# Gate and up products of two feed-forwards by seven products of halves, with negated halves and adding transfers

## The reference

```python
def swiglu(h, w_gu, w_down):
    gu = h @ w_gu
    g, u = jnp.split(gu, 2, axis=-1)
    return (jax.nn.silu(g) * u) @ w_down
...
        x = x + swiglu(rms_norm_2(x, ffn_norm[l]), ffn_w_gu[l], ffn_w_down[l])
```

## Time and profile before

| | us |
|---|---|
| median of 3 runs | 1973.48 (1969.23 to 1978.84) |
| the profiled execution | 1978.27 |
| its span, first to last instruction | 1976.5 |
| busy: TensorE, weight loads | 1916.9, 1540.9 |
| busy: VectorE, ScalarE, POOL | 1328.6, 1024.8, 197.5 |

### The profile page before, as it was taken

How to read it: one execution, slowest core, us unless ns; L and a number is a source line. 1 busy time by engine, 2 the same in 40 slices (tenths; PEclk the granted TensorE clock), 3 DMA queues, 4 the chain that set the end, 5 groups by cost and what they waited for, 6 DMA issues and landing times.

```text
span 1976.5 us, 23049 instructions
## 1 busy us (share of the span) xinstructions
PE 1916.9 (97%) x8818; PEld 1540.9 (78%) x8818; DVE 1328.6 (67%) x1698; ACT 1024.8 (52%) x1562; POOL 197.5 (10%) x261
## 2 busy tenths in 40 slices
PE   5999999999999999999999999999999999999997
PEld 4768868888888888758888888887777778888886
DVE  6776699998999999863542844748445452745737
ACT  4434258888888888744332422426555542332423
POOL 4110221122211100020000000000020100000000
PEclk9999999999999999999999999999999999999999
DMA  8556479999999999962233052322221134052211
GB/s 282 165 195 217 157 262 355 377 374 379 381 366 370 362 363 366 339 205 70 64 128 128 1 192 64 110 82 78 96 64 65 43 116 131 21 192 64 83 66 43
DMA packets 200026, 366.50 MB, mean 185 GB/s; under 512 B 13514, under 2 KB 84055, under 8 KB 199914
## 3 DMA queue, kind: packets, MB, share of 16 engines
q1 hardware_dynamic: 181152, 343.20, 49.4%
q10 hardware_dynamic: 8714, 11.17, 1.7%
q0 software_dynamic: 10048, 10.62, 1.6%
HBM read 365.05 MB, written 24.65 MB: 197 GB/s over the span
## 4 chain that ended last, share of the span: by engine, by line
PE 85%; DVE 7%; DMA 3%; issue 2%; ACT 2%; POOL 1%; ACTq 0%; POOLq 0%; DVEq 0%
PE ps L361 82%; DVE wlo L306 3%; DMA raw<-in_w_expert_gate 1%; PE ps L2323 1%; DMA VR<-in_b_subln 1%; PE ps L2350 1%; ACT whi L277 1%; DMA raw<-in_w_expert_up 0%; DMA raw<-in_w_expert_down 0%; PE ps L3150 0%; DMA raw<-in_a_w_in 0%; PE ps L898 0%; DVE acc L358 0%; DVE X L2937 0%; DMA raw<-in_ada_w 0%
## 5 line engine op out<-in xcount | busy, mean ns | idle before, releaser
L306 DVE TENSOR_TENSOR wlo<-raw,whi 128x1024 fp32r<-128x1024 f32 (+1 forms) x598 | 697.8, 1212 | 228.2 <-ACT whi L277 224.6
L277 ACT ACTIVATE whi<-raw 128x1024 fp32r<-128x1024 f32 (+1 forms) x598 | 594.1, 1045 | 279.6 <-PE ps L361 248.0
L361 PE MATMUL ps<-hT3h,whi 128*128 128x512 f32 x352 | 137.2, 390 | 0.6 <-DVE hT3l L358 0.6
L361 PE MATMUL ps<-hT5h,whi 128*128 128x512 f32 x352 | 137.2, 390 | 0.6 <-DVE hT5l L358 0.6
L361 PE MATMUL ps<-hT3h,wlo 128*128 128x512 f32 x352 | 137.1, 390 | 0.0
L361 PE MATMUL ps<-hT3l,whi 128*128 128x512 f32 x352 | 137.1, 390 | 0.0
L361 PE MATMUL ps<-hT5h,wlo 128*128 128x512 f32 x352 | 137.1, 389 | 0.0
L361 PE MATMUL ps<-hT5l,whi 128*128 128x512 f32 x352 | 137.1, 389 | 0.0
L2960 DVE TENSOR_TENSOR XN<-XN,ps 128x512 f32<-128x512 f32 x44 | 30.1, 688 | 129.1 <-PE ps L361 128.5
L2892 ACT ACTIVATE XN<-ps 128x512 f32<-128x512 f32 x44 | 26.3, 597 | 164.8 <-PE ps L361 163.0
L361 PE MATMUL ps<-whi,XT1h 128*128 128x512 f32 x256 | 102.8, 402 | 1.5 <-DVE XT1l L2406 1.5
(11 more groups left out here) (491 smaller groups left out, 4183.5 us busy)
## 6 DMA issues: line engine op xcount, KB each, us to landing
raw<-in_w_expert_gate SPq DMA_DIRECT2D x64, 1024.0 KB, 7.3
raw<-in_w_expert_up SPq DMA_DIRECT2D x64, 1024.0 KB, 8.1
raw<-in_w_expert_down SPq DMA_DIRECT2D x64, 1024.0 KB, 7.2
raw<-in_ffn_w_gu SPq DMA_DIRECT2D x44, 1024.0 KB, 5.1
raw<-in_ffn_w_down SPq DMA_DIRECT2D x16, 1024.0 KB, 8.8
raw<-in_ada_w SPq DMA_DIRECT2D x24, 512.0 KB, 4.8
raw<-in_a_w_in SPq DMA_DIRECT2D x8, 1024.0 KB, 11.0
raw<-in_kv_w SPq DMA_DIRECT2D x8, 1024.0 KB, 5.2
```

The costliest lines, as they stand in the source:

```text
L277: e.activation(hi[:, c], x, ACT.Copy).then_inc(self.S("w_hi"), 1)
L306: e.tensor_tensor(lo[:, c], raws[h], hi[:, c].bitcast(F32), ALU.subtract).then_inc(self.S("w_lo"), 1)
L361: return e.matmul(o, l, r, start=start, stop=stop, skip_group_check=True)
```

## The change

The first unit of each feed-forward stays as it was. The other ten (`up`, n = 1 to 10) are done by seven products of halves too: tokens in two halves (EARLY_T, tokens 256 to 511; LATE_T, 0 to 255), the contraction of 1024 in two halves of 4 chunks, and columns in up and gate. Product p takes 4 weight chunks x 2 stationary chunks x 3 = 24 matmuls, 256 tokens wide. Products 1, 6, 7 and 4 share one bank (z), 5 and 3 another (v), 2 a third (y). Between products ScalarE copies z after 1, v after 5 and z after 6, and VectorE adds v and z onto these copies after 3 and 7 and y after 2 (`gather`); two silus and two gates (`gate`) follow. A product that goes on in a bank waits until the copy or the gather of that bank is done.

The sums of activations for products 5, 6, 7 and 3 are made once for a layer, during unit 0: four whole operands from high and low, three sums, and four roundings and subtractions (`SUMS`, `SX12`, `SX3`; product 3's take the place of the late half of `hT3`).

Sums of weights, for the down groups too, are now made so: ScalarE negates block b12 in place (`negate_over`); POOL's transfer adds b11 to it from HBM (`add_first`, sum 1, product 5); VectorE adds b22 (`add_total`, sum 2, product 6); ScalarE negates b11 after product 1 was split (`negate_first`), and writes the negated total over b12 after product 5 was split (`negate_total`); two more transfers of POOL add the total to b11 (sum 3, product 7) and b21 to b12 (sum 4, product 4). So of four block operations of VectorE one stays, and three negations and three transfers are added, in 13 *quads* per layer: 10 units and 3 down groups.

Raw buffers are 0 to 3 for everything. Splits of `up` are of 1024 elements and go over six half places; down splits keep three whole ones. The down product's left operand has three slots, not four. The distance matrix follows the last quad's sum 3 (its space holds sums now), the final gain is loaded by SP after the last quad. Some semaphores are merged.

```diff
--- before.py
+++ after.py
...
+    def negate_over(self, e, q):
+        items, _, _ = self.quads[q]
+        e.wait_ge(*self.loaded(items[1][0]))
+        for x in self.block(q, 1):
+            m = e.activation(x, x, ACT.Copy, scale=-1.0)
+        m.then_inc(self.S("negated"), 1)
...
+    def negate_total(self, e, q):
+        _, _, made = self.quads[q]
+        e.wait_ge(*self.lowered(made[5]))
+        e.wait_ge(self.S("sum2"), q + 1)
+        for out_, x in zip(self.block(q, 1), self.total(q)):
+            m = e.activation(out_, x, ACT.Copy, scale=-1.0)
+        m.then_inc(self.S("negated"), 1)
+    def add_total(self, e, q):
+        items, _, _ = self.quads[q]
+        before = q - 1 if self.wide(q) or q > 0 and self.wide(q - 1) else q - 2
+        e.wait_ge(*self.loaded(items[3][0]))
+        e.wait_ge(self.S("sum1"), 16 * (q + 1))
+        if before >= 0:
+            e.wait_ge(self.S("negated"), 3 * before + 3)
+            e.wait_ge(self.S("sum3"), 16 * (before + 1))
+            e.wait_ge(*self.lowered(self.quads[before][2][6]))
+        for out_, x, y in zip(self.total(q), self.block(q, 3), self.block(q, 1)):
+            m = e.tensor_tensor(out_, x, y, ALU.add)
+        m.then_inc(self.S("sum2"), 1)
...
+    def add_first(self, e, q):
+        items, a, _ = self.quads[q]
+        i, at = items[0]
+        first = self.items[i] if at is None else self.items[i][:, at * a:(at + 1) * a, :]
+        e.wait_ge(self.S("negated"), 3 * q + 1)
+        e.dma_start(self.block(q, 1, False)[0].rearrange("p (c n) -> p c n", c=a), first, accum_op=ALU.add).then_inc(self.S("sum1"), 16)
+    def add_rest(self, e, q):
+        items, _, _ = self.quads[q]
+        e.wait_ge(self.S("negated"), 3 * q + 2)
+        e.wait_ge(self.S("sum2"), q + 1)
+        e.dma_start(self.block(q, 0, False)[0], self.total(q, False)[0], accum_op=ALU.add).then_inc(self.S("sum3"), 16)
+        e.wait_ge(self.S("negated"), 3 * q + 3)
+        e.wait_ge(*self.loaded(items[2][0]))
+        e.dma_start(self.block(q, 1, False)[0], self.block(q, 2, False)[0], accum_op=ALU.add).then_inc(self.S("sum4"), 16)
...
+            def columns(n):
+                order = (0, DFF) if n == 0 else (DFF, 0)
+                return [W.item(up[:, :, n * 256 + m:n * 256 + m + 256]) for m in order]
+            for name, i in zip("gu", columns(0)):
+                W.split(f"f{name}{l}", i, 8, 256)
+            spare_user[l] = W.last_in(3)
+            n = 1
             for f0, fn in FG:
                 a = fn // 2
-                pairs, quad = [], []
...
+                W.places = [4, 5, 6, 7, 8, 9]
+                while 2 * n < f0 + fn:
+                    fu, fg = columns(n)
+                    W.quad(f"up{l}", ((fg, 0), (fu, 0), (fg, 1), (fu, 1)), 4, ORDER)
+                    n += 1
+                W.places = [0, 1, 2]
+                over, first, right, low = ((W.item(down[:, f0 + k:f0 + k + a, h:h + 512]), None)
+                                           for k, h in ((0, 512), (0, 0), (a, 512), (a, 0)))
                 W.quad(f"fd{l}", (first, over, low, right), a, ORDER)
...
+        def rows_in(hT, p):
+            kc, ts = {1: (0, EARLY_T), 2: (4, EARLY_T), 3: (0, LATE_T), 4: (4, LATE_T)}.get(p, (0, None))
+            if ts is None:
+                return [x[:, :, :] for x in {5: SX12[0], 6: SX12[1], 7: SX3}[p]]
+            return [x[:, kc:kc + 4, ts] for x in hT]
...
+            def up(n, m, p):
+                j = up_pieces(l, n)[m]
+                w, x = W.parts(j), rows_in(hT, p)
+                b = R.claim(e, f"up{l}.{n}.{p}")
+                e.wait_ge(*W.lowered(j))
+                if n == 1 and p in SUM_ORDER:
+                    e.wait_ge(S("left_lo"), 16 + left_before(l) + SUM_ORDER.index(p) + 1)
+                for k in range(2):
+                    for kc in range(4):
+                        i = mm3(e, b[:, k * 256:(k + 1) * 256], [y[:, kc, k * P:(k + 1) * P] for y in w], [y[:, kc, :] for y in x],
+                                k == 0 and kc == 0 and p in (1, 5, 2), kc == 3)
+                i.then_inc(*R.fill(f"up{l}.{n}.{p}"))
...
+            def up(n, m, p):
+                at = chunks(n)
+                if p == 1:
+                    copy(n, p, FA[:, at, EARLY_T])
+                if p == 5:
+                    if n > 1:
+                        e.wait_ge(*gated(l, n - 1, 2))
+                    copy(n, p, LATE[1][:, :, :])
+                if p == 6:
+                    copy(n, p, LATE[0][:, :, :])
+                if p == 4:
+                    e.wait_ge(*R.done(f"up{l}.{n}.2"))
+                    e.activation(FA[:, at, EARLY_T], FA[:, at, EARLY_T], ACT.Silu).then_inc(S("silu"), 1)
+                    e.wait_ge(*R.full(f"up{l}.{n}.4"))
+                    e.activation(FA[:, at, LATE_T], two(R.bank(f"up{l}.{n}.4")), ACT.Silu).then_inc(*R.free(f"up{l}.{n}.4"))
...
+                    for m, p in enumerate(ORDER):
+                        j = up_pieces(l, n)[m]
+                        W.high(e, j + W.depth(j))
+                        if m == 0:
+                            W.negate_over(e, q + 1)
+                        if m == 3 and f < fn - 2:
+                            W.negate_first(e, q + 1)
+                        if m == 5 and f < fn - 2:
+                            W.negate_total(e, q + 1)
+                        if m == 1 and f == 4:
+                            e.wait_ge(*gated(l, n - 1, 2))
+                            high(gi, f0, a, 0)
+                        if m == 2 and f == fn - 2:
+                            e.wait_ge(S("s_sum"), summed(l, gi, 1))
+                            high(gi, f0, a, 1, 0, a - 2)
+                        if f == 0 and m == 0:
+                            e.wait_ge(S("left_lo"), splits(l, gi - 1, 6))
+                        up(n, m, p)
...
+                W.negate_first(e, q)
                 for m in range(2, 7):
                     W.high(e, js[m] + 1)
                     if m < 5:
-                        e.wait_ge(S("s_sum"), 5 * gi + m + 1)
+                        e.wait_ge(S("s_sum"), summed(l, gi, m + 1))
                     high(gi, f0, a, m)
-                if f0 + fn == 22:
+                    if m == 2:
+                        W.negate_total(e, q)
+                    if m == 3 and f0 + fn < 22:
+                        W.negate_over(e, q + 1)
...
+            def gather(n, p, x):
+                e.wait_ge(*R.full(f"up{l}.{n}.{p}"))
+                e.wait_ge(*R.done(f"up{l}.{n}.{({3: 6, 7: 5, 2: 1})[p]}"))
+                e.tensor_tensor(x, x, two(R.bank(f"up{l}.{n}.{p}")), ALU.add).then_inc(*R.free(f"up{l}.{n}.{p}"))
+            def gate(n, part):
+                ts, p = ((EARLY_T, 3), (LATE_T, 7))[part - 1]
+                x = FA[:, chunks(n), ts]
+                e.wait_ge(*((S("silu"), (UNITS - 1) * l + n) if part == 1 else R.done(f"up{l}.{n}.4")))
+                e.wait_ge(*R.done(f"up{l}.{n}.{p}"))
+                e.tensor_tensor(x, x, LATE[part - 1][:, :, :], ALU.mult).then_inc(S("gated"), 1)
...
+                        if m == 3 and f < fn - 2 or m == 6 and f == fn - 2:
+                            W.add_total(e, q + 1)
+                        W.low(e, max(j + 1, j + W.depth(j) - (1 if m in (3, 4, 5) else 0)))
+                        if m == 0 and f > 0 and n > 1:
+                            gate(n - 1, 2)
+                        if m == 0 and f == fn - 2:
+                            cs = slice(0, a - 2)
+                            e.wait_ge(*gated(l, n - 1, 2))
+                            e.tensor_tensor(a21[:, cs, :], a21[:, cs, :], a22[:, cs, :], ALU.add).then_inc(S("s_sum"), 1)
+                        if m == 1 and f == 4:
+                            low(gi, a, 0)
+                        if m == 2 and f == fn - 2:
+                            low(gi, a, 1, 0, a - 2)
+                        if p == 3:
+                            gather(n, p, LATE[0][:, :, :])
+                        if p == 7:
+                            gather(n, p, LATE[1][:, :, :])
+                        if p == 2:
+                            gather(n, p, FA[:, chunks(n), EARLY_T])
+                        if p == 4:
+                            gate(n, 1)
...
+                        if m == 4:
+                            W.add_total(e, q)
                         if m < 6:
-                            W.low(e, js[m] + 4)
+                            W.low(e, js[6] + (3 if m == 4 else 5))
...
+        def ffn_pool(e, l):
+            for q in range(13 * l, 13 * l + 13):
+                if q % 13 > 0:
+                    W.add_first(e, q)
+                W.add_rest(e, q)
```

463 lines of the change are left out of this document (275 added, 188 removed).

## The result

The changed kernel takes 1993.34 us as the median of four runs (1991.81 to 1993.46), the kernel before 1973.15 (1969.23 to 1978.84): ratio 1.0098, 95% interval 1.0073 to 1.0124. The change makes it 20 us, 1%, **slower**. 1960 and "faster" were forecast, so the direction was wrong.

What follows compares the result with a forecast made beforehand. TensorE, busy 97% of the span, was taken as the bound. Matmuls gain 47.9 us, waits in down groups and unit 1 cost 34.3: -13.6, so 1960 us against a median of 1973.48, range 1935 to 2015.

Steps and rivals of the forecast that it cites:

- The matmuls: In 20 gate/up units, 168 matmuls of 256 columns at 0.115 us replace 96 of 512: 47.9 us gained.
- short matmuls dearer: Rival for the up products: 256-column matmuls take 0.122 us each, the gain is 24 us, total 1984; chance 8%.
- Unit 1's start: First copy of product 1's bank in unit 1 comes late, done at 6 us, wanted at 5.5: 0.5 us, twice.
- The down groups: TensorE waits there for VectorE's order and a negation behind a load: 33.3 us over both layers, possibly 8 to 55.
- The adding transfers: POOL's 512 KB adding transfers take 6.5 us; up to 8.8 is free, beyond it each us costs one in 20 units.
- slow adds: Rival: adding transfers of 12 us delay ScalarE's rounding for product 7 in every unit, 64 us more, 2024; chance 17%.
- The other engines: VectorE gets 125 us more work in all and ScalarE some 200; both fit beside TensorE in a unit.
- Loads not hidden: Rival: a weight load starts only after the matmul before it ends, about 0.224 us each, 318 more, 2278; chance 1%.

Runs made afterwards that it cites:

- d1_busy_gap: The changed kernel, with TensorE multiplying a unit matrix into a free bank during the four waits before product 7: 1981.53 us.
- t1_add_delayed: Changed kernel with ScalarE's next-unit negation after product 2's rounding, plus one plain 512 KB transfer delaying the adding transfers of products 7 and 4: 2032.3 us.

## Why the prediction was wrong

By its own steps, in the order of its sum:

1. *The matmuls*, 47.9 us gained at 0.115. Measured 0.120: 434.3 - 20 x 168 x 0.120 = 31.1. This is the first failed step, 17 us. Its reason, "a long matmul does not pay for its load, and a short one need not either" from the earlier trace rows, holds in its first half (0.2333 against 0.2304) and fails in its second: at 256 columns a narrower load takes 6.7 ns off. And the half of 0.2262 from which 0.115 was taken halves a part that does not shrink: beside their columns at 2.4 GHz both widths pay 13 ns. The measured 0.120 lies inside the forecast's own bounds (0.111 to 0.122), near the end that the ten 128-column matmuls gave. The rival "short matmuls dearer" names the effect, at 0.122 and with 8%. The Trainium skill's 109 ns (TensorE: Matmul & The Clock Gate, Back-to-back issue gap) was 11 too low here.
2. *Unit 1's start*, 0.5 us twice: none in the first layer, 1.4 in the second, at the copy named, against 1.0 in all. Near in sum, though not in its two halves.
3. *The down groups*: right in place, nearly in size. Waits of the first group 10.6 and 9.4 us (7.7 forecast), of the second 7.1 (5.3), of the third 3.2 (4.25); 40.7 in all against 34.5 (33.3 went into the sum, which took off 0.6 us a layer for waits of before that its text gives as half a microsecond). Product 1 waited 1.5 of 1.6 forecast. Two terms were too small. The load was given 6.0 us and took 8.7 in the first group of the first layer, 7.4 in the other three. And products 6 and 3 waited 1.3, not 0.6, since the forecast had them wait for their left operand, while each also takes over a bank that VectorE must first add to X (L3145), one instruction later.
4. *The halved clock* was no term at all: 8 to 12 us, as d1_busy_gap shows, 9.9 by the stretches at half clock. The trace of before had no half clock inside the feed-forwards, so the gaps were priced by their length alone. This is the second failed step, a term put at nothing without a reason: ahead of the feed-forwards the same trace has a gap of TensorE with a half clock behind it (lines behind this list), so its price could have been asked for. Without the halved clock the changed kernel takes 1981.5 (d1_busy_gap), still no gain.
5. *The adding transfers*: 6.5 us taken for 512 KB, 6.0 and 6.1 measured; no wait in units 2 on, as said. The reason behind it, room up to 8.8, was about 2 us too wide by the estimate from t1_add_delayed, since it left the first transfer of a unit out, and the kernel was near the rival "slow adds" without a sign of it. The Trainium skill (Collectives: The Full Stack, The bandwidth ceiling) puts the adding step of a collective over several cores at half the rate of its copying step; taken over to these single transfers that would have been 9.0, and the trace disagrees.
6. *The other engines*: 125 us more for VectorE and 200 for ScalarE were forecast; 121 and 186 came.
7. *Loads not hidden* (1%) didn't come: a load of 128 columns and a matmul of 256 follow each other every 0.120 us. Its price was mis-added: 2278 is 1960 + 318, and 1960 already has the 47.9 us gained, so it should have been 2326.

A gap of TensorE in the trace of before, and the window behind it:

```profile
846.35 2.22 PE L361 MATMUL ps<-XN,DG 128*128 128x512 f32 x3 [3.29 <-issue]
...
847.00:850.50 3.50, 3.50 (x6) 1.38 (x5) 0.00 (x0) 0.00 (x0) 0.00 (x0) 0.51 1.03 359
```

In sum: -31 + 1.4 + 41 + 10 is +21, less 2 that the rest of the kernel gained (why is not known), against 19.7 measured. From the forecast's -13.6 the spacing takes 17 us, the halved clock 10 and the longer waits 7 (40.7 against 33.3). The spacing alone would have left +3, the halved clock alone -4, neither of which can be told from none; together with the waits they turned the sign. A forecast of waits of 5 us at four places was right there, and should have raised the question of what TensorE does after standing still.

What the change is worth: with one negation moved, 1957.87, 0.8% less than the kernel before. That this is within 2 us of the forecast is luck: the long waits, which the forecast counted, are gone, and the matmuls gain 17 us less.

## What to carry to other kernels

Halving the columns of a matmul doesn't halve its time: read the fixed part from two widths before the saved multiplications are counted; here 13 ns at 128-column loads, an eighth on top of what 256 columns take at 2.4 GHz. When an in-order engine gets an instruction that waits for a transfer, list what stands behind it and put it as late as its reader allows; the load can take just as long. Price a TensorE gap of some us with the clock behind it, and an instruction that hands a bank on with the product that takes it over.
